# First expert pair's rows placed by one-hot matmuls from x on chip, and last pair's rows placed and all rows summed in PSUM, in a one-core hybrid encoder layer

## Chip, cores and metric

The kernel runs on one core of a Trainium2 chip. The metric is the device time of one execution in microseconds (us). Everything is float32. The kernel is written engine by engine with semaphores, so each engine executes its own list in the order in which the code is written: PE (matmul), DVE (vector), ACT (scalar), POOL (GpSimd) and SP, whose queue issues most of the transfers.

## The reference, cut to what matters

512 prompt tokens and 64 sample tokens of width 1024 (576 rows, five tiles: four of 128 rows and one of 64) pass one encoder layer. The change touches its last part, the mixture of experts, and the final norm:

```python
# router: top-1 of 4 groups, then top-2 of the 8 experts of that group
g_idx = jnp.argmax(glog, axis=-1)
top_v, top_i = lax.top_k(elog_g, 2)
gate = jax.nn.softmax(top_v, axis=-1) * g_w[:, None]
e_idx = g_idx[:, None] * 8 + top_i
# per expert, on the rows that chose it (h = rms_norm(x)); 32 experts, FF = 512
y = (silu(h @ w_gate[e]) * (h @ w_up[e])) @ w_down[e]
x = x + sum_over_the_2_experts(gate * y)
y_out = rms_norm(x, final_norm_g)
```

## The kernel before, in words

Attention, the HGRN2 recurrence, memory attention and the router take the first 640 us of the span. Then come 16 "pairs" (PAIRS). A pair is two experts, each with room for 64 rows (CAP), so its operand is one 128-row tile: columns 0 to 63 are the rows of one expert and 64 to 127 those of the other. Rows past 64 of an expert go into "over" passes after pair 8. Experts 0 to 3 are always pairs 0 and 1, so these two can start before the order of the rest is known.

**Weights.** Each pair needs six parts of 2 MB (two gate, two up, two down), 16 x 6 in all, streamed by SP through ten slots (PART, `load_part`). Part q goes into the slot of part q-10, so it waits until PE has read that one (`freed`): up parts of pair i free the slots for the gate parts of pair i+2, down parts of pair i those for its up parts, gate parts of pair i+1 those for its down parts. Pair 1's down parts are an exception: they go in halves, the first when PE has read half of pair 0's gate parts (`g_half`), the second after `g_full` (L1098 to L1104). Pair 15's parts go in quarters (`load_quarters`).

**Rows.** As the last projection gives x tile by tile (`proj_N(16, ...)`), ACT stores it to DRAM (`store_x`), PE turns it for the router (`turn_x`, `router`), and DVE chooses the experts (`choose`). `ranks` counts on PE which place a row has in its expert. For the first two pairs, DVE makes one-hots of the places (`near_slots`, `near_values`) and PE multiplies them with the token numbers (`near_tokens`), which gives the list of rows. POOL gathers these rows of x from DRAM (L1233) into `xg`, PE turns them (`turn_rows`) and DVE copies them, times the norm's gain, into `xgT` (`copy_rows`). Lists for the other pairs come from a second chain: about 9 us of small DVE steps up to `order_ready` (L1961 to L1990), 8 us more up to the one-hots (L2001 to L2057), ten matmuls on PE (`all_lists`, L916), and `read_lists` (`table_ready`), after which POOL may gather pair 2's rows.

**A pair** on PE: gate and up (`from_rows`, 16 matmuls each), `turn_rows` of the next pair, `turn_h`, down (`by_both`). ACT takes exp of the gate, DVE makes the swish (`swish_rows`), copies the turned product, and adds the gated result to the rows (`drain_rows`); the rows a token has for its first expert carry x itself (`own_rows`). POOL scatters the 128 rows to DRAM (`expert_rows`, one half for each of a token's two experts) and gathers the rows of pair i+3. PE's down of pair i waits until DVE has drained pair i-1 (`y_cp`).

**The end.** After pair 15's scatter has landed, SP and ACT load both halves of `expert_rows` (ten transfers), DVE adds them (L2122), ACT squares and sums, POOL takes the inverse root, DVE scales (L2127), SP stores.

Of the kernel before, what the change touches and what calls it, by code (L numbers as in the profile page):

```python
# [14 lines left out]
F32 = mybir.dt.float32  # L15
I32 = mybir.dt.int32
# [31 lines left out]
NOROW = 4096  # L48
PAIRS = NE // 2
# [55 lines left out]
def encoder(nc, a, outs):  # L105
# [4 lines left out]
    with ExitStack() as ctx:  # L110
# [6 lines left out]
        banks = [ctx.enter_context(nc.psum_tensor(f"bank{i}", [P, 512], F32)) for i in range(6)]  # L117
# [73 lines left out]
        x_sb = area(XZ, NT, 1024)  # L191
        hmT = area(Z2, KC, TOK)
# [16 lines left out]
        xgT = area(44032, KC, P)  # L209
        eG = area(OZ, 512)  # L210
        hET = area(OZ + 512, 4, P)
        hE = area(OZ + 1024, 512)
        hE_rows = hE.rearrange("p (d k) -> p k d", k=4)
        gS2 = area(OZ + 1536, 512)
        yS = [area(OZ + 2048 + 1024 * i, 1024) for i in range(2)]
        xo = area(OZ + 4096, 1024)
        xo_rows = xo.rearrange("p (d k) -> p k d", k=KC)

        yg = [[area(1024 * (2 * t + k), 1024) for k in range(2)] for t in range(NT)]
# [59 lines left out]
        r_g1 = early(NT)  # L279
        r_sum = early(NT)  # L280
# [3 lines left out]
        r_t = early(NT, NE)  # L284
        r_sel = early(NT, NE)
        before = early(NT + 1, NE)
        place = early(NT, NE)
# [6 lines left out]
        rank4 = early(NT, 4)  # L294
        own4 = early(NT, 4)
        valid4 = early(2, NT, 4)
        pair4 = early(2, NT, 2)
        list4 = early(2, NT, 2, 2)
# [3 lines left out]
        kept = scratch(OZ + 2048, OZ + 5376)  # L302
        oh = kept(2, NT, NE)
        hot_s = kept(2, NT, P)
        order_cmp = area(OZ + 2048 + 2 * NT * NE, NE, NE)
        cmp_e = area(OZ + 2048 + 2 * NT * NE, OVER, NE)
        squares4 = area(OZ + 2048 + 2 * NT * (NE + P), 1024)
        hot_p = kept(2, NT, NB // 2)
        lists = kept(2, NT, 4, NB // 2)
        lo_f = kept(2, NT)  # L310
        hi_f = kept(2, NT)
        eo = kept(OVER)
        cmp_p = kept(OVER)
        npf = kept(1)
# [3 lines left out]
        r_x4 = kept(NT, 4)  # L318
# [15 lines left out]
        half4 = fixed(4)  # L334
# [4 lines left out]
        ocol = fixed(4)  # L339

# [49 lines left out]
        near_hot, near_full, near_ready, near_std = (sem(f"near_{n}") for n in ("one_hots", "lists_full", "rows_ready", "std_ready"))  # L390
        hot_ready, lists_full, table_ready, order_ready = (sem(f"list_{n}") for n in ("one_hots", "full", "table_ready", "order_ready"))
# [13 lines left out]
        over_done = sem("over_passes_done")  # L405
        gf_ld = sem("final_gain_loaded")
        yg_ld = [sem(f"y_rows_loaded{t}") for t in range(NT)]
        fsum, fssq, frstd, fin_ready = (sem(f"final_{n}") for n in ("sum", "ssq", "rstd", "ready"))
        fin_st = sem("final_stored")

        A = PsumRing(banks[0:3], a_full, a_free)
# [49 lines left out]
        def _(pe):  # L461
# [345 lines left out]
            def near_tokens(a, b):  # L807

                for k in range(2):
                    for t in range(a, b):  # L810
                        rows = TILES[t][1]
                        ins = mm(near_list, hot_s[0:rows, k, t, :], list4[0:rows, k, t].rearrange("p v i -> p (v i)"), start=k == 0 and t == 0,
                                 stop=k == 1 and t == SAMPLE, skip_group_check=True)
                return ins
# [24 lines left out]
            router(3, HIGH)  # L839
            turn_x(4, 1)  # L840
            router(4, HIGH)
            pe.wait_ge(near_hot, 1)
            near_list = A.open(pe)[:, 0:4]
            mark["near"] = A.filled % 3
            near_tokens(0, 2)
            pe.wait_ge(sel_ready, 2)
            ranks(2, NT)
            pe.wait_ge(near_hot, 2)
            near_tokens(2, NT).then_inc(near_full, 1)

            pe.wait_ge(v_free, V.filled)
            pe.wait_ge(a_free, A.filled)
# [22 lines left out]
            def from_rows(S, n, bank, w, signal, half_read=None):  # L875

                for k in range(KC):
                    if k % 4 == 0:
                        pe.wait_ge(S.xT_cp, 2 * n + k // 4 + 1)
                    for j in range(2):  # L880
                        own = slice(CAP * j, CAP * (j + 1))
                        ins = mm(bank[own, :], xgT[:, k, own], w[j][:, k, :], start=k == 0, stop=k == KC - 1)  # L882
# [41 lines left out]
            for i in range(PAIRS):  # L924
# [20 lines left out]
                if i == 0:  # L945
                    all_lists()
# [1210 lines left out]
```

## Time and profile before

| | |
|---|---|
| Time, median of 3 | 1164.77 us (1164.1 to 1165.12) |
| The profiled execution | 1165.38 us, its span 1163.6 us |
| PE, PEld, DVE, ACT, POOL busy | 89%, 46%, 39%, 16%, 10% of the span |
| Read from HBM | 273.34 MB, of which 96 expert parts of 2048 KB and six more for the over pass |
| The chain that ended last | PE 69%, DMA 18%, DVE 6%, SP's queue 4% |

The span can be read in three stages: up to about 650 us PE is nearly always busy and the transfers mostly idle; from about 662 us to 1120 us the 16 DMA engines are full; the last 30 us follow the last weights. In a table of `--windows` kind the columns are the stretch, its length, then the busy time of PE, PEld, DVE, ACT and POOL with the count of instructions, the granted TensorE clock (1.00 is 2.4 GHz, 0.50 is 1.2 GHz), the busy share of the DMA engines and GB/s. In a timeline they are start, duration, engine, line, operation, out<-in with shapes, count, and in brackets the idle time before and who ended it. A float32 matmul counts as two PE instructions in the trace and as one in the listings of order.

### The profile page before, as it was taken

To read this page: it belongs to the slowest core of one execution; us is meant where nothing else is said; L and a number is where in the kernel's file an instruction comes from. 1 tells how busy PE (TensorE), PEld (TensorE's weight loads), DVE (VectorE), ACT (ScalarE), POOL (GpSimd) and SP (SyncE) were. 2 spreads that over 40 slices of the span, in tenths; PEclk is the share of its full clock that TensorE was granted. 3 is DMA by queue.
4 is the path that set the end of the run, shared out by engine and by line. 5 is a ranking of instruction groups with operands and counts; after the bars stand their busy time and mean duration, and the time that the engine had idled before them with its cause. 6 is when DMAs were issued, how large, how long until landed. Compare 5 with 4: busy or idle time off the path is not lost.

```text
span 1163.6 us, 11497 instructions
## 1 busy us (share of the span) xinstructions
PE 1032.4 (89%) x4528; PEld 540.7 (46%) x4528; DVE 458.5 (39%) x770; ACT 186.1 (16%) x486; POOL 113.1 (10%) x167
## 2 busy tenths in 40 slices
PE   6999999999999999999998699987876889887880
PEld 3577744555445446777656343333332233333320
DVE  4169645563664024013227743322222233322224
ACT  0156233433113101012101000000000000000001
POOL 1200001132016000000000010010000000100002
PEclk9999999999999999999998699999989899989995
DMA  8221130312233433212085599999999999999977
GB/s 254 73 73 54 45 123 1 134 52 82 74 108 103 177 145 145 73 57 89 1 355 200 220 397 427 427 427 426 428 427 426 422 427 427 426 427 427 413 297 251
DMA packets 56548, 277.50 MB, mean 238 GB/s; under 512 B 13360, under 2 KB 15280, under 8 KB 44336
## 3 DMA queue, kind: packets, MB, share of 16 engines
q1 hardware_dynamic: 43648, 256.01, 54.7%
q10 hardware_dynamic: 7808, 11.32, 2.7%
q0 software_dynamic: 5040, 9.45, 2.2%
q8 instruction: 36, 0.59, 0.2%
q14 instruction: 16, 0.13, 0.0%
HBM read 273.34 MB, written 18.61 MB: 251 GB/s over the span
## 4 chain that ended last, share of the span: by engine, by line
PE 69%; DMA 18%; DVE 6%; SPq 4%; issue 2%; ACT 0%; POOL 0%; ACTq 0%; DVEq 0%; POOLq 0%
PE bank L497 23%; DMA arena<-in_exp_w_down_dram 15%; PE bank L485 13%; PE bank L882 12%; PE bank L872 6%; SPq L1089 4%; PE bank L501 2%; PE bank L747 2%; PE score_pair L721 2%; PE bank L635 1%; DVE arena L1675 1%; DMA arena<-expert_rows 1%; PE score_pair L551 1%; PE bank L585 1%; DMA arena<-in_w_in_dram 1%
## 5 line engine op out<-in xcount | busy, mean ns | idle before, releaser
L497 PE MATMUL bank<-arena 128*128 128x512 f32 x640 | 285.0, 599 | 2.6 <-DMA arena<-in_w_in_dram 1.9
L882 PE MATMUL bank<-arena 128*64 128x512 f32 x1024 | 238.3, 622 | 38.5 <-issue 35.2
L497 PEld LDWEIGHTS bank<-arena 128*128 128x128 f32 x640 | 119.7, 191 | 147.0 <-issue 145.5
L882 PEld LDWEIGHTS bank<-arena 128*64 128x64 f32 x1024 | 83.4, 143 | 190.6 <-issue 189.4
L485 PE MATMUL bank<-arena 128*128 128x288 f32 x640 | 156.1, 406 | 0.0
L872 PE MATMUL bank<-arena 128*64 128x512 f32 x512 | 119.5, 621 | 26.6 <-DMA arena<-in_exp_w_down_dram 19.5
L485 PEld LDWEIGHTS bank<-arena 128*128 128x128 f32 x640 | 121.4, 190 | 33.8 <-issue 0.4
L1298 ACT ACTIVATE arena<-bank 128x512 f32<-128x512 f32 (+6 forms) x135 | 61.7, 493 | 378.3 <-PE bank L497 112.5
L872 PEld LDWEIGHTS bank<-arena 128*64 128x64 f32 x512 | 39.9, 142 | 95.1 <-issue 83.5
L1521 ACT ACTIVATE arena<-bank,arena 128x512 f32<-128x512 f32 x17 | 11.7, 687 | 428.3 <-PE bank L882 404.4
L2045 DVE SCALAR_TENSOR_TENSOR arena<-bank,arena 128x512 f32<-128x512 f32 x34 | 25.5, 751 | 109.8 <-PE bank L872 102.8
L2028 DVE TENSOR_SCALAR arena<-arena 128x512 f32<-128x512 f32 x17 | 7.3, 427 | 131.9 <-ACT arena L1521 131.9
L2030 DVE RECIPROCAL arena<-arena 128x512 f32<-128x512 f32 x17 | 57.0, 3353 | 0.6
L1237 POOL DMA_INDIRECT expert_rows<-arena,ints x17 | 17.2, 1010 | 384.3 <-DVE arena L2045 383.7
L1795 DVE TENSOR_TENSOR arena<-arena,bank 128x512 f32<-128x512 f32 x16 | 11.0, 688 | 87.0 <-PE bank L497 68.1
L1142 POOL TENSOR_SCALAR arena<-arena 128x1 f32<-128x1 f32 (+4 forms) x31 | 8.9, 288 | 373.4 <-ACT arena L1403 225.1
L1712 DVE SCALAR_TENSOR_TENSOR arena<-arena,score_pair 128x256 f32<-128x256 f32 (+4 forms) x20 | 15.3, 764 | 64.7 <-PE score_pair L551 49.3
L2035 DVE SCALAR_TENSOR_TENSOR arena<-bank,arena 128x512 f32<-128x512 f32 x17 | 12.8, 751 | 59.4 <-PE bank L882 55.6
L1775 DVE SCALAR_TENSOR_TENSOR arena<-arena,bank 128x128 f32<-128x128 f32 x68 | 23.7, 348 | 29.5 <-PE bank L635 26.5
L1825 DVE TENSOR_REDUCE arena<-score_pair 128x4 f32<-128x1024 f32 (+1 forms) x5 | 6.1, 1225 | 69.1 <-PE score_pair L721 69.1
L501 PE MATMUL bank<-arena 128*64 128x256 f32 x256 | 29.5, 382 | 0.5 <-DVE arena L1837 0.5
L1413 ACT ACTIVATE arena<-arena 128x128 f32<-128x128 f32 (+4 forms) x40 | 21.3, 534 | 35.5 <-DVE arena L1716 35.5
(295 smaller groups left out, 928.1 us busy)
## 6 DMA issues: line engine op xcount, KB each, us to landing
arena<-in_exp_w_gate_dram SPq DMA_DIRECT2D x30, 2048.0 KB, 33.0
arena<-in_exp_w_up_dram SPq DMA_DIRECT2D x30, 2048.0 KB, 37.7
arena<-in_exp_w_down_dram SPq DMA_DIRECT2D x28, 2048.0 KB, 34.7
arena<-in_w_in_dram SPq DMA_DIRECT2D x7, 2048.0 KB, 8.5
out_dram<-arena SPq DMA_DIRECT2D x4, 1024.0 KB, 10.5
arena<-in_w_mem_k_dram SPq DMA_DIRECT2D x2, 2048.0 KB, 10.3
arena<-in_w_mem_v_dram SPq DMA_DIRECT2D x2, 2048.0 KB, 8.6
arena<-in_w_out_dram SPq DMA_DIRECT2D x2, 2048.0 KB, 12.7
```

The lines of the kernel that those rows point to most:

```text
L485: ins = mm(b[:, 0:HALF], w[:, k, c * P:(c + 1) * P], src[:, k, t0:t0 + HALF], start=k == 0, stop=k == KC - 1)
L497: ins = mm(b[:, :], x, w[:, k, :], start=k == 0, stop=k == KC - 1)
L501: ins = mm(b[rows * half:rows * (half + 1), 0:256], x, w[:, k, 256 * half:256 * (half + 1)], start=k == 0, stop=k == KC - 1)
L721: ins = mm(o, qmT[:, 2 * h + c, t0:t0 + rows], keys[:, 2 * h + c, :], start=c == 0, stop=c == 1)
L747: ins = mm(b[:, c * P:c * P + rows], vals[:, m, j * P:(j + 1) * P], pT[:, 2 * (j // 2) + m, 0:rows], start=m == 0, stop=m == 1)
L872: ins = mm(bank[own, :], x[:, k, own], w[j][:, k, cols], start=k == 0, stop=k == nk - 1)
L882: ins = mm(bank[own, :], xgT[:, k, own], w[j][:, k, :], start=k == 0, stop=k == KC - 1)
L1089: sp.dma_start(pass_weights(i)[2 * which + j][:, ks, :], weights_of(which, e[j])[:, ks, :]).then_inc(late_ld[which][k], 16)
L1298: A.done(f(dst, get(b), ACT.Copy))
L1775: ins = stt(out=dst, in0=state(g), scalar=EB[:, h, g:g + 1], in1=inc, op0=ALU.mult, op1=ALU.add)
L2030: v.reciprocal(eG, eG).then_inc(S.chain, 1)
L2045: stt(out=y[:, cols], in0=banks[3 + half][:, :], scalar=gates, in1=own[:, cols], op0=ALU.mult, op1=ALU.add).then_inc(S.y_cp, 1)
```

## The change

It has two parts, and the moves that make room for them.

**First pair.** `ranks` now puts -1024 (PICKED) on the diagonal of its triangle, so that the rank of a chosen row is marked by itself, and DVE makes the one-hots of a tile in one comparison (`near_rows`; three calls for tiles 0-1, 2, 3-4 in place of `near_slots` and `near_values` for tiles 0-1 and 2-4). PE multiplies x, still in SBUF and read in columns, by the one-hot: `place_x(t, ks)` adds tile t's part of the first pair's operand, already turned, into two banks; eight matmuls of 128 columns for each of five tiles. Neither the gather, nor `turn_rows` of pair 0, nor the DVE order chain stands ahead of pair 0 any more. The gather of pair 0 is still issued, for `own_rows`. DVE now goes on with `order_ready`'s chain, then `swish_rows` of pair 0, `copy_rows` of pair 1, the second chain, `all_lists`, `read_lists`, `passes_needed`, and only then `drain_rows` of pair 0. PE runs `all_lists` in pair 1 (after its up matmuls, ahead of `turn_rows` of pair 2) instead of in pair 0. `copy_rows` of pair 0 waits for all stores of x, and SP's part (1, 3) for PE's reading of x tile 0.

**Last pair.** The 1152 rows of `expert_rows` are zeroed in DRAM early (four transfers of SP, from a zeroed stretch of SBUF, when `pool_c` is 2, ahead of `load_unit(2)`). Pair 15 is not scattered. Its 128 rows stay in SBUF; DVE makes a one-hot of their tokens (`hot_last`), and PE adds, in PSUM and for each of the five token tiles, the one-hot product (`place_last`) and the two loaded halves multiplied by the identity (`add_loaded`): two plus four matmuls of 512 columns a tile, 30 in all. The loads now wait for pair 14's scatter only, and all ten are issued by SP. ACT and DVE read the sums from PSUM.

PE around pair 0 before (L804 ranks, L778 turn_x, L792 router, L812 near_tokens, L857 turn_rows, L882 gate and up, L916 all_lists, L864 turn_h, L872 down):

```order
L792 MATMUL score_pair<-arena 128x36 x4
L778 MATMUL bank<-arena 128x64 x4
L792 MATMUL score_pair<-arena 64x36 x4
L812 MATMUL bank<-arena 128x4 x4
L803 MATMUL bank<-arena 128x128
L804 MATMUL bank<-arena 128x96
L812 MATMUL bank<-arena 128x4 x6
L857 MATMUL score_pair<-arena 128x128 x8
L882 MATMUL bank<-arena 64x512 x32
L857 MATMUL score_pair<-arena 128x128 x8
L916 MATMUL bank<-arena 128x100 x10
L864 MATMUL bank<-arena 128x128 x4
```

The same place now (L829 place_x, L821 near_tokens, L912 gate and up):

```order
L829 MATMUL banks<-arena 128x128 x4
L787 MATMUL banks<-arena 128x64 x4
L829 MATMUL banks<-arena 128x128 x4
L801 MATMUL score_pair<-arena 64x36 x4
L829 MATMUL banks<-arena 128x128 x16
L821 MATMUL score_pair<-arena 128x2 x6
L812 MATMUL banks<-arena 128x96
L813 MATMUL banks<-arena 128x64
L829 MATMUL banks<-arena 128x128 x16
L821 MATMUL score_pair<-arena 128x2 x4
L912 MATMUL banks<-arena 64x512 x32
```

The turning of gathered rows ahead of the first gate and up is gone, and 40 matmuls of 128 columns have come in.

PE in pair 1 now, from its gate and up to pair 2's (L887 turn_rows of pair 2, L946 all_lists, L894 turn_h, L902 down):

```order
L912 MATMUL banks<-arena 64x512 x32
L946 MATMUL banks<-arena 128x100 x10
L887 MATMUL score_pair<-arena 128x128 x8
L894 MATMUL banks<-arena 128x128 x4
L902 MATMUL banks<-arena 64x512 x16
```

Between the lists and down stands the turning of pair 2's rows, which are gathered by these lists.

DVE from the end of the order chain to the drain of pair 0, now, with the steps inside each chain left out (L2068 to L2077 swish_rows, L2020 copy_rows, L2116 the last one-hots, L2130 to L2138 read_lists, L2154 the end of passes_needed, L2111 drain_rows):

```order
L2063 CAST ints<-arena 128x32
L2068 TENSOR_SCALAR arena<-arena 128x512
L2077 COPY arena<-banks 128x512
L2020 TENSOR_TENSOR arena<-score_pair,arena 128x512 x2
L2116 TENSOR_TENSOR arena<-arena 128x640
L2130 TENSOR_SCALAR ints<-banks 128x25
L2138 TENSOR_SCALAR arena<-banks 128x25
L2154 CAST ints<-arena 128x1
L2111 SCALAR_TENSOR_TENSOR arena<-banks,arena 128x512 x2
L2068 TENSOR_SCALAR arena<-arena 128x512
```

Before, the second chain stood ahead of pair 0's swish; the swish of pair 1 (the last row) now stands behind the lists' reading and pair 0's drain.

PE after the last down now (L936 down by quarters, L1016 place_last, L1025 add_loaded; before, its list ends with down):

```order
L936 MATMUL banks<-arena 64x512 x16
L1016 MATMUL banks<-arena 128x512
L1016 MATMUL score_pair<-arena 128x512
L1016 MATMUL banks<-arena 128x512 x4
L1025 MATMUL banks<-arena 128x512 x4
L1025 MATMUL score_pair<-arena 128x512 x4
L1025 MATMUL banks<-arena 128x512 x8
L1016 MATMUL banks<-arena 64x512 x2
L1025 MATMUL banks<-arena 64x512 x4
```

The 30 matmuls follow down, those of the loaded rows behind the placed ones of the first four tiles.

The diff, cut to its core:

```diff
+            def place_x(t, ks):
+                rows = TILES[t][1]
+                for k in ks:
+                    ins = mm(first_rows[k // 4][:, (k % 4) * P:(k % 4 + 1) * P], x_cols[t][0:rows, k, :], near_hots[0:rows, t, 0, :],
+                             start=t == 0 and k % 4 == 0, stop=t == SAMPLE, skip_group_check=True)
+                return ins
             router(3, HIGH)
+            pe.wait_ge(sel_ready, 2)
+            ranks(2, 3)
+            pe.wait_ge(a_free, A.filled)
+            pe.wait_ge(near_hot, 1)
+            place_x(0, LOW)
             turn_x(4, 1)
+            place_x(0, HIGH).then_inc(x0_read, 1)
             router(4, HIGH)
+            place_x(1, range(KC))
+            pe.wait_ge(near_hot, 2)
+            place_x(2, range(KC))
+            near_tokens(0, 3)
+            pe.wait_ge(sel_ready, 3)
+            ranks(3, NT)
+            pe.wait_ge(near_hot, 3)
+            for ks in (LOW, HIGH):
+                place_x(3, ks)
+                place_x(4, ks).then_inc(SP_.tx_full, 1)
+            pe.wait_ge(near_hot, 4)
+            near_tokens(3, NT).then_inc(near_full, 1)
...
-            pe.wait_ge(xg_ld[0], 16)
-            turn_rows(SP_, xg_rows[0])
...
+                if i == 0:
+                    pe.wait_ge(near_std, 1)
+                if i == 1:
+                    all_lists()
                 if i + 1 < PAIRS and i != OVER_AFTER:
                     pe.wait_ge(xg_ld[(i + 1) % 3], 16 * ((i + 1) // 3 + 1))
                     turn_rows(SP_, xg_rows[(i + 1) % 3])
-                if i == 0:
-                    all_lists()
...
+            for half in range(2):
+                pe.wait_ge(SP_.y_cp, 2 * PAIRS - 1 + half)
+                for t in range(2):
+                    place_last(t, half)
+            for t in range(2, SAMPLE):
+                for half in range(2):
+                    place_last(t, half)
+            for t in range(SAMPLE):
+                add_loaded(t)
+            pe.wait_ge(fin_ready, 1)
+            for half in range(2):
+                place_last(SAMPLE, half)
+            add_loaded(SAMPLE)
...
+            sp.wait_ge(pool_c, 2)
+            y_flat = y_dram.rearrange("(p r) n -> p (r n)", p=P)
+            for c in range(4):
+                sp.dma_start(y_flat[:, 2304 * c:2304 * (c + 1)], area(OZ, 2304)).then_inc(y_zero, 16)
...
-            sp.wait_ge(y_st[1], 16 * (PAIRS // 2))
+            sp.wait_ge(y_st[1], 16 * (PAIRS // 2 - 1))
...
+            swish_rows(SP_, 0, 0, near[:, 1, 0:1])
+            copy_rows(SP_, 1, turned)
...
             all_lists()
+            read_lists()
+            passes_needed()
+            n.settle()
             for i in range(PAIRS):
-                swish_rows(SP_, i, 0, near[:, 1, 0:1] if i == 0 else table[:, 1, i:i + 1])
+                if i > 0:
+                    swish_rows(SP_, i, 0, table[:, 1, i:i + 1])
+                    if i + 1 < PAIRS and i != OVER_AFTER:
+                        copy_rows(SP_, i + 1, turned)
```

## Rows read from the trace of the kernel before

**Rows 1.** Table of stretches: busy times, granted clock, DMA share, GB/s.

```profile
646.50:661.72 15.22, 8.55 (x26) 3.83 (x28) 13.95 (x48) 0.07 (x1) 2.31 (x2) 0.52 0.24 75
684.38:707.66 23.28, 22.50 (x110) 8.33 (x108) 8.67 (x9) 1.72 (x2) 2.41 (x3) 1.00 0.99 404
752.00:1120.00 368.00, 304.08 (x1360) 118.02 (x1356) 109.47 (x112) 22.41 (x26) 25.41 (x30) 0.94 1.01 424
```

**Rows 2.** Timeline, 630 to 662 us: the router's end and pair 0's start.

```profile
630.04 1.08 PE L792 MATMUL score_pair<-arena 128*128 128x36 f32 x8
633.74 0.16 DVE L1892 TENSOR_REDUCE arena<-arena 128x2 f32<-128x8 f32 x1
...
638.47 0.42 DVE L1906 TENSOR_TENSOR arena<-arena 128x32 f32<-128x32 f32 x2
642.48 2.99 PE L812 MATMUL bank<-arena 128*128 128x4 f32 x12 [2.36 <-DVE arena L1932]
651.25 1.97 PE L857 MATMUL score_pair<-arena 128*128 128x128 f32 x8 [5.78 <-DMA arena<-x_rows,ints]
654.22 0.18 DVE L1990 CAST ints<-arena 128x32 int32<-128x32 f32 x1
655.14 16.84 PE L882 MATMUL bank<-arena 128*64 128x512 f32 x64 [1.92 <-DVE arena L1997]
661.72 4.24 SPq L1104 DMA_DIRECT2D arena<-in_exp_w_down_dram  x4
```

**Rows 3.** The chain that ended last, merged: start, length, what.

```profile
538.53 3.57 PE bank L747 x32
595.05 6.87 PE bank L497 x16
684.34 13.73 PE bank L882 x64
773.19 8.78 PE bank L872 x32
```

**Rows 4.** Timeline, 672 to 693 us: pair 0's lists, table, gather.

```profile
672.91 2.88 PE L916 MATMUL bank<-arena 128*128 128x100 f32 x20
677.25 7.09 PE L872 MATMUL bank<-arena 128*64 128x512 f32 x32 [0.78 <-DVE arena L2037]
677.90 0.18 DVE L2071 TENSOR_SCALAR arena<-bank 128x25 f32<-128x25 f32 x1
678.85 0.99 POOL L1233 DMA_INDIRECT arena<-x_rows,ints x1 [29.55 <-DVE arena L2071]
681.81 0.15 DVE L2087 CAST ints<-arena 128x1 int32<-128x1 f32 x1
684.38 0.82 SPq L1047 DMA_DIRECT2D arena<-in_exp_w_up_dram  x2
692.44 3.35 DVE L2030 RECIPROCAL arena<-arena 128x512 f32<-128x512 f32 x1
```

**Rows 5.** DMA issues, us to landing: at 679 us, 684 us, all 18.

```profile
arena<-x_rows,ints POOLq DMA_INDIRECT x1, 7.3
arena<-x_rows,ints POOLq DMA_INDIRECT x1, 10.1
arena<-x_rows,ints POOLq DMA_INDIRECT x18, 15.3
```

**Rows 6.** The chain that ended last, from 1133 us.

```profile
1133.06 0.75 DVE arena L2045
1139.44 13.20 DMA arena<-expert_rows
1156.25 1.06 ACT arena L1554
```

**Rows 7.** Timeline, POOL near 36 us.

```profile
35.66 0.54 POOL L1167 MEMSET arena<- 128x20 f32 x1
```

**Rows 8.** Table of stretches, 36 to 48 us.

```profile
36.00:48.00 12.00, 12.00 (x57) 5.92 (x57) 3.23 (x17) 1.50 (x4) 0.20 (x1) 1.00 0.01 1
```

More of the change, by code:

```diff
@@ L48 @@
 NOROW = 4096
+PICKED = 1024.0
 PAIRS = NE // 2
@@ L191, in encoder @@
         x_sb = area(XZ, NT, 1024)
+        x_cols = [x_sb[:, t, :].rearrange("p (d k) -> p k d", k=KC) for t in range(NT)]
         hmT = area(Z2, KC, TOK)
@@ L405, in encoder @@
         over_done = sem("over_passes_done")
+        y_zero, count_ready, hot_last_ready = sem("y_rows_zeroed"), sem("token_count_ready"), sem("last_one_hot_ready")
+        f_full = sem("tokens_summed")
         gf_ld = sem("final_gain_loaded")
         yg_ld = [sem(f"y_rows_loaded{t}") for t in range(NT)]
-        fsum, fssq, frstd, fin_ready = (sem(f"final_{n}") for n in ("sum", "ssq", "rstd", "ready"))
+        fssq, frstd, fin_ready = (sem(f"final_{n}") for n in ("ssq", "rstd", "ready"))
         fin_st = sem("final_stored")
+        summed = [bank_pairs[0], pair, bank_pairs[1], bank_pairs[2], bank_pairs[0]]
         A = PsumRing(banks[0:3], a_full, a_free)
@@ L807, in near_tokens @@
             def near_tokens(a, b):
[L809 to L813, printed above, removed]
+                for t in range(a, b):
+                    rows = TILES[t][1]
+                    for i in range(2):
+                        ins = mm(near_list[:, 2 * i:2 * i + 2], near_hots[0:rows, t, i, :], near_vals[0:rows, t, :], start=t == 0 and i == 0,
+                                 stop=t == SAMPLE, skip_group_check=True)
+                return ins
+            def place_x(t, ks):
+                rows = TILES[t][1]
+                for k in ks:
+                    ins = mm(first_rows[k // 4][:, (k % 4) * P:(k % 4 + 1) * P], x_cols[t][0:rows, k, :], near_hots[0:rows, t, 0, :],
+                             start=t == 0 and k % 4 == 0, stop=t == SAMPLE, skip_group_check=True)
                 return ins
@@ L980, in _, with place_last, add_loaded @@
                     turn_rows(SP_, xg_rows[(i + 1) % 3])
+            pe.wait_ge(hot_last_ready, 1)
+            def place_last(t, half):
+                t0, rows = TILES[t]
+                mm(summed[t][0:rows, half, :], hot_last[:, t0:t0 + rows], yS[(PAIRS - 1) % 2][:, 512 * half:512 * (half + 1)],
+                   start=True, stop=False, skip_group_check=True)
+            def add_loaded(t):
+                rows = TILES[t][1]
+                pe.wait_ge(yg_ld[t], 32)
+                for half in range(2):
+                    for k in range(2):
+                        ins = mm(summed[t][0:rows, half, :], ident[0:rows, 0:rows], yg[t][k][0:rows, 512 * half:512 * (half + 1)],
+                                 start=False, stop=k == 1, skip_group_check=True)
+                ins.then_inc(f_full, 1)
+            for half in range(2):
[8 more added lines that the diff above has]
+            pe.wait_ge(fin_ready, 1)
+            for half in range(2):
+                place_last(SAMPLE, half)
+            add_loaded(SAMPLE)
         @block.sync
@@ L1547, in _ @@
                     over_loop(act, over_pair)
-            act.wait_ge(y_st[0], 16 * (PAIRS // 2))
-            act.wait_ge(y_st[1], 16 * (PAIRS // 2))
-            for t, (t0, rows) in enumerate(TILES):
-                act.dma_start(yg[t][1][0:rows, :], y_dram[TOK + t0:TOK + t0 + rows, :]).then_inc(yg_ld[t], 16)
             for t, (_, rows) in enumerate(TILES):
-                act.wait_ge(fsum, t + 1)
-                f(yg[t][1][0:rows, :], yg[t][0][0:rows, :], ACT.Square, accum_out=ssq[0:rows, 17 + t:18 + t]).then_inc(fssq, 1)
+                act.wait_ge(f_full, t + 1)
+                f(yg[t][1][0:rows, :].rearrange("p (h n) -> p h n", h=2), summed[t][0:rows, :, :], ACT.Square,
+                  accum_out=ssq[0:rows, 17 + t:18 + t]).then_inc(fssq, 1)
         @block.vector
```

206 lines of the change are left out of this document (100 added, 106 removed).

## Prediction

> **What bounds the kernel now.** I read the page's busy slices first, then stretches, the chain that ended last, and the timeline at the two places of the change. From 752 to 1120 us the DMA engines have a busy share of 1.01 and move 424 GB/s, while PE is idle for 64 of 368 us: the weights' transfer sets the time there [rows 1]. From 684.38 us, while PE is still ahead of its weights, the share is 0.99 already. But from 646.5 to 661.72 us, it is 0.24: all slots are full and SP waits for the first half of pair 0's gate to be read. So what counts at the start is when that happens (661.72 us, the issue of L1104 [rows 2]), and whether the engines run dry later. At the end it is what lies behind the last weights: drain at 1133.06 us, scatter, load for 13.20 us, sums, norm, store [rows 6]. The profiled execution took 1165.38 us with a span of 1163.6, and is 0.6 us above the median; I sum on it and take 0.6 off.
>
> **Zeroed rows.** SP issues them when POOL's constants are ready, after 35.66 + 0.54 = 36.2 us [rows 7]. From 36 to 48 us the DMA share is 0.01 [rows 8]. 4.7 MB at 424 GB/s are 11.1 us, done by 47.5 us. The weights behind them in SP's queue wait for PE to have read its first unit, which by the idle engines isn't before 48 us, and PE then has the second unit to work on. Cost 0; if the writes took double, still 0.
>
> **Pair 0's start.** A 128-column matmul costs 3.57 us / 16 = 0.223 us at the full clock (32 instructions are 16 matmuls) [rows 3]. PE is through the last projection at 630.1 us. Router 1.1 us (its row: 1.08), ranks of tile 2 0.65, four placings 0.9, turning 0.5, four placings 0.9, router 0.7: the fifth tile's logits are full at 634.8 us, some 2 us later than before. DVE takes them and chooses for tiles 3 and 4, 5.15 us from 633.74 to 638.89 before [rows 2], now 635.1 to 640.3. Placing tiles 1 and 2 (16 x 0.223 = 3.6 us) and six near_tokens lie on PE beside that. Then ranks 0.7, the comparison 0.5, placing tiles 3 and 4 16 x 0.223 = 3.6, four near_tokens. Those cost 2.99 / 6 = 0.5 us each in the row at 642.48 us, where the clock was 0.5 [rows 2]; at the full clock I take 0.3. Sum 646.3, with semaphores 647 us, against 655.14. Half of the gate's matmuls are a quarter of the 13.73 us of a pair's 64 instructions at the full clock [rows 3], 3.4 us; before, the clock was 0.52 on average over this stretch [rows 1], and it took 6.6. SP issues at 650.7 us instead of 661.72: **-11.0 us** at the start of the full stream. The bounds: -12 if no hop costs anything; -2.5 with PE at 1.2 GHz in the last placings (rival C).
>
> Parts (1,2) and (1,3) change places and wait for the logits and for tile 0's placing, both by 635 us, when part (1,0), issued at 630.2, still fills the engines: 0.
>
> **Pair 0 and what it pushes back.** The shift is handed on to the end only if the engines never run dry. From 647: gate and up to 660.8. DVE's order chain runs from 646.5 for the 8.7 us that it took before (to 654.22 plus 0.18 [rows 2]), so the swish starts at 655.4, waits a little for up, and down 0 runs from 663.7 to 670.8 (7.09 us [rows 4]). Each issue up to there follows the one before closely enough: 0.
>
> The second list chain used to be hidden beside pair 0's gate and up. Its lists are now summed on PE in pair 1. Pair 1's gate and up take 13.8 us, to 684.6; the ten list matmuls 2.9 (20 instructions [rows 4]), to 687.5; the table is ready 1.0 later and POOL's gather starts 0.8 after that (677.90 + 0.18 to 678.85 [rows 4]): 689.3 us. Only when it has landed can PE turn pair 2's rows, and turn_h and down of pair 1 stand behind that in PE's list. Before, this gather was issued in pair 0 and PE never waited for it. Now nothing hides it. Its landing is the price that the trace doesn't fix: alone it took 7.3 us at 679 and 10.1 at 684 us, and the median of all 18, most of them behind a scatter, is 15.3 [rows 5]. The new one stands alone, but with about 15 us of weights queued ahead, as at no place of before. I take 10.1: 699.4 us. PE has then been idle for 12 us, so its clock will be at 1.2 GHz: turning 1.97 us (the row at 651.25 [rows 2]), turn_h 1.3, DVE's copy 0.7, down 8.78 as after another long wait (773.19 [rows 3]): it ends at 712.3 us. Parts (3,2) and (3,3) wait for it.
>
> How long can the engines go on? At 670.8 us six parts' worth is still to come before those two: 12.58 MB at 424 GB/s are 29.7 us; with three gathers and a scatter of 0.52 MB each 5.0 more: dry at 705.5 us. From 684.38 to 707.66 us the rate was 404 [rows 1], which makes it 707. Idle **+7.0 us**, of which the bounds are +4 (landing at 696.6, then the swish of pair 1 is what is late) and +12 (15.3).
>
> The Trainium skill ("DMA: Bandwidth & Descriptors", Queues, rings and completion order) says that each engine takes turns between its queues packet by packet; a lone gather would then land in some 4.5 us by its fixed 2 us and its rate, an estimate of mine from that page's figures. The landings in rows 5 speak against it, and by the rule the sum would be that of rival A.
>
> After that DMA catches up and DVE and POOL have no late work: nothing in pairs 2 to 14 changes.
>
> **The end.** The last quarter of down and the two drains stay as they are. Placing may start when the first drain is done (1133.06 + 0.75, so 1133.9 us). Thirty matmuls of 512 columns at 6.87 / 8 = 0.859 us [rows 3] are 25.8 us; the sample tile's, with 64 output rows, have as many columns and cost the same. PE has been busy before, so I take the full clock. Loads: SP issues them when pair 14's scatter has landed, behind the last quarters in the same queue, and these have landed before 1133 us. 4.7 MB are 11.1 us, so the first tile lands by 1135.3 and the last by 1144. PE wants the first at 1133.9 + 8 x 0.859 = 1140.8 and one more each 3.4 us: hidden. All sums are in PSUM at 1159.7 us. Before, the last sum was ready at 1156.25 us, when ACT squared it [rows 6]. Square, inverse root, scaling and store follow as before, 7.4 us; a read of 1024 columns from PSUM I price at up to 0.2 us more in all. **+3.5 us**, bounds +2.8 and +4.5. Scatter, DVE's adds and the load go, but what takes their place is longer: PE must do six passes over every row behind the drain, four of which (the loaded rows) didn't need it.
>
> Sum: -11.0 + 7.0 + 3.5 = -0.5 us. 1165.38 - 0.5 - 0.6 gives **1164.3 us**: no change that can be told (about 0.2%, 2.3 us, is what a measurement of this kernel tells from none).
>
> **Rivals.**
> A, faster: the gather lands in 7.3 us or less. Then pair 1's swish is late: table 688.5, passes_needed 2.6 (681.96 less 678.08, less 1.3 for the copy that stood between [rows 4]), pair 0's drain 1.6 (two of 0.75 [rows 6]), swish 5.3 around the 3.35 us reciprocal [rows 4]: 698.1, down ends at 709.4, idle 4.0. With the start 0.5 us better the sum is -11.5 + 4.0 + 3.5 = -4.0: 1160.8. For it: the 7.3 us; against it: that one had a short queue ahead. 34%.
> B, slower: the gather lands like the others, 15.3 us: down ends at 717.5, idle 12, sum +4.5: 1169.3. For it: the queue is as deep as in the steady pairs; against: no scatter ahead. 16%.
> C, slower: PE is at 1.2 GHz when tiles 3 and 4 are placed. Before, it was there from 634 us on, after small router matmuls and waits. Then ranks, 16 placings, four near_tokens cost 0.7 + 3.6 + 0.8 more and the first half gate 3.4: the start gives only -2.5, and the sum is +8.0: 1172.8. It decides from the point where PE idles before sel_ready 3. Against: the placings of tiles 1 and 2 keep it at work until 640 us. 10%.
> D: the end at 1.2 GHz, 25.8 us more, and 1190. PE has no long pause before it. 2%.
> That the change doesn't do what it says: the listings show the gather gone from pair 0's way. 2%, with the times of before.
>
> **How the numbers follow.** Forecast 36%. The case without effect is within 0.2% too, but the forecast's upper edge passes it, so same stays at 36%. Faster: A, 34%. Slower: B, C, D and that edge, 30%. The range goes from A's better half to between B and C: 1159.3 to 1171. The forecast's own, with an idle time of 5 to 9 us: 1162.3 to 1166.3.
>
> **What the profile would show.** Pair 0's gate starting near 647 us at a clock near 1, and no turning before it; a wait of about 10 us of PE for x_rows in pair 1, the clock at 0.5 after it, and a dip in DMA share near 706 to 712 us; 30 matmuls in the last 30 us and ACT's last square 3 to 4 us later behind the last drain than before (23.2 us). If the last quarter of down lands 4 us earlier, both start terms hold. Wrong it would be if the dip isn't there (faster), or if pair 0 starts after 650 us (slower).

## The result and the profile after

The changed kernel takes **1178.3 us** (median of 4 runs, 1175.55 to 1180.25), the kernel before 1164.64 beside it: a ratio of 1.0118, 95% interval 1.0101 to 1.0134. The forecast, 1164.3 with a range to 1171, was wrong, its range too. The profiled execution took 1176.76 us with a span of 1175.0, against 1163.6 before: 11.4 us to find. (The medians are 13.7 us apart: the profiled execution of before is 0.7 us above its median, that of the changed kernel 1.5 us below. No profile shows the other 2.3 us.)

First pair 0's start, the timeline of the changed kernel (start, length, engine, line, what; [idle before it and who ended that]):

```profile
630.89 2.14 PE L829 MATMUL banks<-arena 128*128 128x128 f32 x8
635.56 1.07 PE L801 MATMUL score_pair<-arena 128*64 128x36 f32 x8
636.55 7.90 PE L829 MATMUL banks<-arena 128*128 128x128 f32 x32
644.29 1.40 PE L821 MATMUL score_pair<-arena 128*128 128x2 f32 x12
646.71 8.88 PE L829 MATMUL banks<-arena 128*128 128x128 f32 x32 [0.52 <-DVE arena L1990]
657.40 15.80 PE L912 MATMUL banks<-arena 128*64 128x512 f32 x64
662.95 4.25 SPq L1170 DMA_DIRECT2D arena<-in_exp_w_down_dram  x4
```

L829 places rows of x. Eight instructions took 2.14 us while the clock was still up, 0.27 us each, where the forecast had 0.11 (0.223 a matmul, which is two instructions). The gate (L912) starts at 657.4 instead of 647, and 2.3 us later than before [rows 2]. SP issues at 662.95, 1.2 us later than before, not 11.0 earlier.

The clock over this stretch (us, PE busy, granted clock, DMA share, GB/s):

```profile
632.00:634.00 2.00, 2.00 (x12) 0.97 0.97 410
634.00:636.00 2.00, 2.00 (x11) 0.50 0.98 410
638.00:640.00 2.00, 2.00 (x10) 0.50 0.73 266
642.00:644.00 2.00, 2.00 (x10) 1.00 1.08 455
646.00:648.00 2.00, 1.48 (x7) 0.88 0.96 410
648.00:650.00 2.00, 2.00 (x9) 0.50 0.08 33
```

The clock falls to 1.2 GHz twice: at 634 us, when PE has been busy without a gap, and at 647 us, after a wait of 0.52 us. At 642 to 644 us, with the clock at 2.4 GHz, it does 10 instructions in 2 us, as many as at 638 to 640 with 1.2: something other than the clock holds a placing back.

Then pair 1, where the changed kernel sums the lists (L946), gathers pair 2's rows (L1303) and turns them (L887):

```profile
696.43 2.98 PE L946 MATMUL banks<-arena 128*128 128x100 f32 x20
701.26 0.99 POOL L1303 DMA_INDIRECT arena<-x_rows,ints x1 [39.96 <-DVE arena L2138]
712.45 1.97 PE L887 MATMUL score_pair<-arena 128*128 128x128 f32 x8 [13.04 <-DMA arena<-x_rows,ints]
716.06 7.09 PE L902 MATMUL banks<-arena 128*64 128x512 f32 x32 [0.79 <-DVE arena L2077]
723.18 0.81 SPq L1112 DMA_DIRECT2D arena<-in_exp_w_up_dram x2
```

PE waits 13 us for a gather that lands 11.2 us after POOL's issue. Down 1 ends at 723.1, where the forecast had 712.3: 10.4 of these 10.8 us are the late gate. The rest is small because misses cancel: the gather's issue is 1.6 us later behind the gate than forecast and its landing takes 1.1 us more, but the turning and down 1 take 2.2 us less, as down 1 runs at the full clock (7.09 us) where the forecast had 8.78. The transfers pay for it. Of before, then of the changed kernel (us, granted clock, DMA share, GB/s):

```profile
640.00:730.00 90.00, 0.88 0.86 351
700.00:730.00 30.00, 1.00 1.01 430
```

```profile
640.00:730.00 90.00, 0.84 0.78 316
700.00:730.00 30.00, 0.77 0.80 326
```

Against the 1.01 of full transfer, 90 x (0.86 - 0.78) = 7.2 us of transfer time are lost, 6.3 of them after 700 us. From 730 us both run at 1.01, and the last quarter of down comes 8.0 us later (1139.81 against 1131.84). The end:

```profile
1139.81 1.94 PE L936 MATMUL banks<-arena 128*64 128x512 f32 x8 [0.39 <-DMA arena<-in_exp_w_down_dram]
1141.01 1.54 DVE L2111 SCALAR_TENSOR_TENSOR arena<-banks,arena 128x512 f32<-128x512 f32 x2 [6.09 <-PE banks L936]
1141.90 1.10 PE L1016 MATMUL banks<-arena 128*128 128x512 f32 x2 [0.16 <-DVE arena L2111]
1164.53 3.64 PE L1025 MATMUL banks<-arena 64*64 64x512 f32 x8
```

ACT's last square starts at 1168.21, 27.2 us behind the drain (the row of L2111); before, it was 23.2 (1133.06 to 1156.25, [rows 6]). So 4.0 us; with the 8.0 it makes 12.0, of which 0.6 come back behind the square (6.8 us to the end, 7.4 before): 11.4.

The zeroed rows show as four writes, with a DMA share of 0.58 from 30 to 60 us where it was 0.20, and nothing behind them comes later.

### The profile page after: what moved, and what is told of

It reads as the page before. It is cut to its first block, busy times and chain, and to the rows that moved or that the text cites. A ratio compares the mean times of both kernels' runs of the same rounds, so it can differ in the third digit from the quotient of the medians.

```text
span 1175.0 us, 11766 instructions
## 1 busy us (share of the span) xinstructions
PE 1076.0 (92%) x4664; PEld 565.7 (48%) x4664; DVE 452.4 (39%) x758; ACT 185.6 (16%) x486; POOL 109.1 (9%) x168
## 4 chain that ended last, share of the span: by engine, by line
PE 76%; DMA 13%; SPq 4%; DVE 4%; issue 2%; another core or an unknown queue 1%; ACT 0%; DVEq 0%; POOL 0%; ACTq 0%; POOLq 0%
PE banks L506 23%; PE banks L494 13%; PE banks L912 13%; DMA arena<-in_exp_w_down_dram 11%; PE banks L902 7%; SPq L1155 4%; PE banks L510 2%; PE banks L829 2%; PE banks L756 2%; PE score_pair L730 2%; PE banks L644 1%; PE banks L1025 1%; DVE arena L1745 1%; PE score_pair L560 1%; DMA arena<-x_rows,ints 1%
## 5 line engine op out<-in xcount | busy, mean ns | idle before, releaser
L506 PE MATMUL banks<-arena 128*128 128x512 f32 x640 | 285.2, 599 | 2.5 <-DMA arena<-in_w_in_dram 1.8
L912 PE MATMUL banks<-arena 128*64 128x512 f32 x1024 | 237.1, 620 | 35.8 <-issue 34.3
L506 PEld LDWEIGHTS banks<-arena 128*128 128x128 f32 x640 | 119.8, 191 | 146.9 <-issue 145.4
L912 PEld LDWEIGHTS banks<-arena 128*64 128x64 f32 x1024 | 81.1, 143 | 188.3 <-issue 187.1
L494 PE MATMUL banks<-arena 128*128 128x288 f32 x640 | 156.1, 406 | 0.0
L902 PE MATMUL banks<-arena 128*64 128x512 f32 x512 | 119.2, 620 | 21.2 <-DMA arena<-in_exp_w_down_dram 11.8
L494 PEld LDWEIGHTS banks<-arena 128*128 128x128 f32 x640 | 121.4, 190 | 33.8 <-issue 0.4
L1371 ACT ACTIVATE arena<-banks 128x512 f32<-128x512 f32 (+6 forms) x135 | 61.6, 492 | 378.7 <-PE banks L506 110.5
L902 PEld LDWEIGHTS banks<-arena 128*64 128x64 f32 x512 | 38.4, 142 | 91.1 <-issue 77.7
L2111 DVE SCALAR_TENSOR_TENSOR arena<-banks,arena 128x512 f32<-128x512 f32 x34 | 25.4, 750 | 101.6 <-PE banks L902 95.5
L2068 DVE TENSOR_SCALAR arena<-arena 128x512 f32<-128x512 f32 x17 | 7.2, 426 | 119.0 <-ACT arena L1594 119.0
L2075 DVE SCALAR_TENSOR_TENSOR arena<-banks,arena 128x512 f32<-128x512 f32 x17 | 12.8, 751 | 60.4 <-PE banks L912 57.4
L1845 DVE SCALAR_TENSOR_TENSOR arena<-arena,banks 128x128 f32<-128x128 f32 x68 | 23.6, 348 | 29.5 <-PE banks L644 26.5
L887 PE MATMUL score_pair<-arena 128*128 128x128 f32 x128 | 19.3, 296 | 14.1 <-DMA arena<-x_rows,ints 13.0
L510 PE MATMUL banks<-arena 128*64 128x256 f32 x256 | 29.5, 382 | 0.5 <-DVE arena L1907 0.5
## 6 DMA issues: line engine op xcount, KB each, us to landing
out_dram<-arena SPq DMA_DIRECT2D x4, 1024.0 KB, 10.4
```

The lines of the kernel that those rows point to most:

```text
L494: ins = mm(b[:, 0:HALF], w[:, k, c * P:(c + 1) * P], src[:, k, t0:t0 + HALF], start=k == 0, stop=k == KC - 1)
L506: ins = mm(b[:, :], x, w[:, k, :], start=k == 0, stop=k == KC - 1)
L510: ins = mm(b[rows * half:rows * (half + 1), 0:256], x, w[:, k, 256 * half:256 * (half + 1)], start=k == 0, stop=k == KC - 1)
L902: ins = mm(bank[own, :], x[:, k, own], w[j][:, k, cols], start=k == 0, stop=k == nk - 1)
L912: ins = mm(bank[own, :], xgT[k // 4][:, k % 4, own], w[j][:, k, :], start=k == 0, stop=k == KC - 1)
L1371: A.done(f(dst, get(b), ACT.Copy))
```

## Experiments

The kernel before was timed beside each group of runs: medians 1164.1 to 1164.7. Theory from the first: the placings are slow by themselves and at a low clock (8 us), and the end costs 4.

**only_start** and **only_end** halve the change: the first is the changed kernel with the old end, the second the old kernel with the new end.

> The changed kernel with the end of the kernel before (pair 15 scattered, both halves loaded and added by DVE, no rows zeroed). Theory (the two parts' costs add: the start costs 8 us, by a late pair 0 and a dry stretch of the DMA engines in pair 1; the end 4 us): 1164.6 + 8 = 1172 to 1175 us, pair 1's down ending near 723 us. Rival (the zeroed rows or something between the parts does it, the start alone is harmless): 1164 to 1167 us.

> The kernel before with the end of the changed one alone. Theory: 30 matmuls of 0.86 us behind the first drain, 1164.6 + 4 = 1168.6 us, with a spread as small as before's, since the start is untouched. Rival (the end is harmless, all is lost at the start): 1164 to 1165.5 us.

Only the start: 1173.81 us, ratio 1.0079 (1.0062 to 1.0097); only the end: 1168.01, 1.0029 (1.0016 to 1.0041). The halves add up, 9.7 and 3.9 of 13.7 us. The placings read as in the changed kernel, and ACT's last square of only_end comes 27.2 us behind its drain at 1133.48.

**rows_in_chunks.** A placing's stationary operand took every eighth column of x, a step of 32 bytes. Here it takes 128 neighbouring ones, and pair 0's gate and up weights, and its gain, are read in the matching order.

```diff
-        x_cols = [x_sb[:, t, :].rearrange("p (d k) -> p k d", k=KC) for t in range(NT)]
+        x_cols = [x_sb[:, t, :].rearrange("p (k d) -> p k d", k=KC) for t in range(NT)]
...
+                if i == 0 and m < 4:
+                    src = a[which_name[m // 2]][0, e].rearrange("(k p) n -> p k n", p=P)
```

> The changed kernel with x read by place_x as eight stretches of 128 neighbouring columns instead of every eighth column; pair 0's gate and up parts are loaded, and its gain is taken, in the same order of rows. Theory (the weight loads with a step of 32 bytes take 0.335 us instead of 0.19, they hold the placings at 0.25 us an instruction, and this thin load lets the clock fall): placings of tiles 3 and 4 in 3.6 to 4.5 us instead of 8.9, pair 0's gate at 648 to 651 us, SP's next issue at 652 to 655 instead of 663, time 1167 to 1170 us, runs closer together. Rival (the clock falls for another reason, the step costs nothing): placings as before, 1175 to 1180 us.

1169.69 us (9 runs, 1165.25 to 1172.68), 1.0045 (1.0033 to 1.0058). The time is the expected one; the last placings (3.6 to 4.5 us expected) and a narrower spread didn't come. The placings with x in chunks:

```profile
634.88 3.84 PE L829 MATMUL banks<-arena 128*128 128x128 f32 x32
640.53 0.46 PE L812 MATMUL banks<-arena 128*128 128x96 f32 x2 [0.58 <-DVE arena L1979]
641.71 8.09 PE L829 MATMUL banks<-arena 128*128 128x128 f32 x32 [0.52 <-DVE arena L1993]
651.61 15.70 PE L912 MATMUL banks<-arena 128*64 128x512 f32 x64
```

The weight loads (PEld) of the first eight instructions, in the changed kernel and with x in chunks, both at the full clock:

```profile
630.86 1.98 PEld L829 LDWEIGHTS banks<-arena 128*128 128x128 f32 x8
631.72 0.97 PEld L829 LDWEIGHTS banks<-arena 128*128 128x128 f32 x8
```

Same tile, same count: the step doubles the load, by 0.13 us an instruction. It also goes with the first fall of the clock. From 634 to 640 us both kernels run placings of the same shape with PE busy; the changed kernel, then rows_in_chunks (columns as in [rows 1]):

```profile
634.00:640.00 6.00, 6.00 (x29) 5.71 (x29) 2.82 (x14) 0.00 (x0) 0.00 (x0) 0.50 0.90 322
634.00:640.00 6.00, 5.95 (x56) 5.70 (x54) 4.23 (x21) 0.00 (x0) 0.00 (x0) 1.00 1.01 400
```

The projection before ends up to 0.9 us apart from run to run, so count from the start of the router's last full tile (629.53, here 630.39): the gate starts 27.9 us behind it with the step and 21.2 in chunks, where the forecast had 16.9. So the step costs 6.7 us. The clock is the second fault: it still falls at 641.7 us, after 2-column products and waits of 0.58 and 0.52 us, and the last placing takes 8.09 us for the same 32 instructions.

**clock_kept** and **lists_moved.** The near lists go behind the placings (both); in their place come three products of 512 columns, meant for a free bank (clock_kept alone).

```diff
-near_tokens(0, 3)
+extra(2)        # each: mm(bank, ident, x_sb[:, 2, 0:512])
 pe.wait_ge(sel_ready, 3)
 ranks(3, NT)
+extra(1)
...
-near_tokens(3, NT).then_inc(near_full, 1)
+near_tokens(0, NT).then_inc(near_full, 1)
```

> The kernel with the rows of x read in chunks, and two more edits: the twelve products of the near lists (L821, 1.40 us before the last placings) go behind the placings, and in their place TensorE gets two extra products of 128x128 by 512 columns into a free bank ahead of the ranks and one behind them (0.86 us each at full clock; their result is not used). Theory (the second half of the lost start is the clock, which falls at 641.7 in the chunked kernel after a stretch of 2-column products and waits): the clock stays at 1.00 through the last placings, these take 3.8 to 4.2 us (32 instructions of 0.12) in place of 8.09, the near lists behind them 2.3 in place of 1.96, the first gate half 13.7 in place of 15.70; SP's issue after the gate comes 5 to 7 us before 657.05, and the time is 1163 to 1167 if the stall in pair 1 stays as long (the chunked kernel had 1169.7). Rival 1 (the low clock has nothing to do with what TensorE runs just before): the clock falls in the same place, the last placing takes 8 us, the near lists come behind it, the time is 1170.5 to 1172. Rival 2 (an earlier start is all eaten by the gather's landing): the clock stays up, SP's issue comes earlier, but the pair 1 stall grows by as much and the time stays at 1169 to 1170.

> The same as the kernel before it without the extra products: only the near lists are moved behind the placings. Theory (it is the columns TensorE streams that hold the clock): TensorE now waits from 638.5 to 640.5 for the ranks, the clock falls as in the chunked kernel (0.50 from about 641), the last placing takes 7.5 to 8.1 us, the lists behind it 3 to 4 us more, but a part of that lies beside VectorE's copies; 1169.5 to 1172. Rival (the order is what helped): the clock stays at 1.00 and the time is 1163 to 1167, as with the extra products.

clock_kept holds 2.4 GHz through the last placing:

```profile
636.98 1.88 PE L876 MATMUL banks<-arena 128*128 128x512 f32 x4
639.46 1.08 PE L876 MATMUL banks<-arena 128*128 128x512 f32 x2
640.37 4.31 PE L829 MATMUL banks<-arena 128*128 128x128 f32 x32
644.61 3.14 PE L821 MATMUL score_pair<-arena 128*128 128x2 f32 x20
647.68 16.57 PE L919 MATMUL banks<-arena 128*64 128x512 f32 x64
```

lists_moved, which has PE wait instead:

```profile
640.03 0.53 PE L812 MATMUL banks<-arena 128*128 128x96 f32 x2 [1.86 <-issue]
641.45 8.09 PE L829 MATMUL banks<-arena 128*128 128x128 f32 x32 [0.52 <-DVE arena L1992]
```

So the extra work ahead held the clock, not the order; it fills PE's wait as well, and no run tells the two apart. Behind the placings the clock falls all the same, during the 20 two-column products: 0.57 over 646 to 654 us. The gate takes 16.57 us, more than the 15.70 in chunks, and of the 3.8 us won in the last placing, 1.5 reach its issue, counted from the router. And clock_kept's time is 1170.61 us, 1.0049 (1.0032 to 1.0066), the same as with x in chunks. That is the time of rival 2, though PE's wait for the gather did not grow (12.85 us, 12.75 in chunks). The gate's issue comes 3.1 us earlier (653.99; 1.6 of them because the router was earlier), and so do the gather (692.30) and the turning; then down 1 takes 9.11 us at the low clock in place of 7.09, and the next issue stands at 716.06 against 716.99. Transfers of rows_in_chunks, then of clock_kept:

```profile
640.00:730.00 90.00, 0.85 0.85 344
700.00:730.00 30.00, 0.84 0.82 326
```

```profile
640.00:730.00 90.00, 0.87 0.85 342
700.00:730.00 30.00, 0.82 0.74 297
```

What is won early is lost after 700 us. (In clock_kept and all_mended the extra products fell into the bank of pair 0's first half and overwrite what is placed by then, so these two give wrong rows for pair 0; the instructions are the same, and mended_between below puts them right.) lists_moved took 1175.89 (1172.87 to 1176.02), 4 us above what was expected; its profiled run is the quickest of the four. There the 20 two-column products behind the placings take 4.51 us at the low clock, the gate starts 2.9 us later behind the router than in chunks, and the share over 640 to 730 is 0.82, worth 2.7 us; the rest of the 6 us over rows_in_chunks is open.

**lists_between.** The changed kernel with pair 1's lists between its gate and up, so that the gather lands beside up.

> The changed kernel with PE's list matmuls of pair 1 between its gate and up instead of behind up. Theory (the gather of pair 2's rows stands bare behind the lists and makes the DMA engines run dry): the gather is issued 7 us earlier, pair 1's down ends at 716 instead of 723, the dry stretch shrinks from 6 to 0 us, time 5 to 7 us below the changed kernel, 1170 to 1174 us. Rival (the engines don't miss what they lose there, since the stream is bound later): 1176 to 1180 us.

1172.31 us, 1.0068 (1.0051 to 1.0085): 6.0 us under the changed kernel.

```profile
690.08 2.98 PE L946 MATMUL banks<-arena 128*128 128x100 f32 x20
694.91 0.99 POOL L1303 DMA_INDIRECT arena<-x_rows,ints x1 [32.91 <-DVE arena L2138]
705.80 1.97 PE L887 MATMUL score_pair<-arena 128*128 128x128 f32 x8 [5.72 <-DMA arena<-x_rows,ints]
716.54 0.81 SPq L1112 DMA_DIRECT2D arena<-in_exp_w_up_dram x2
```

The landing is as long, 10.9 us from the issue, but the next issue comes 6.6 us earlier and the share after 700 us is 1.01 again.

**sums_shared.** The old kernel with the new end, in which DVE adds the two loaded halves of each tile as they land, so that PE has 20 products and not 30.

```diff
+tt(yg[t][0], yg[t][0], yg[t][1], ALU.add).then_inc(fsum, 1)     # DVE; slices of rows left out here and below
-    for k in range(2):
-        mm(summed[t], ident, yg[t][k], stop=k == 1)
+    mm(summed[t], ident, yg[t][0], stop=True)
```

> The kernel before with the changed end, in which VectorE adds the two loaded tables of each tile as they land (1.2 us each, five), so that TensorE has 20 products (10 that place, 10 that add) and not 30. Theory (the end was late because it put 25.8 us of TensorE's products behind the last drain): 10 products of 0.86 us fewer, the last square comes 8.6 us earlier than in the changed end alone, the time is 1168.0 - 8.6 = 1159.4, ratio 0.996. Rival (the landing of the ten loads sets the end, 13 to 14 us after an issue at 1131 at the latest, with VectorE's sums behind it): the last sum ends at about 1147 and the products behind it, at most 3 us; that would allow still earlier, so a rival time is only reached if the loads land later than 1152: 1163 to 1166.

1161.21 us (11 runs), 0.9976 (0.9966 to 0.9985): 6.8 us better than the new end, 1.8 less than expected. The rows show most of it:

```profile
1147.18 1.22 DVE L2170 TENSOR_TENSOR arena<-arena 64x1024 f32<-64x1024 f32 x1 [1.04 <-DMA arena<-expert_rows]
1148.33 1.27 DVE L2173 SCALAR_TENSOR_TENSOR arena<-banks,arena 128x1024 f32<-128x1024 f32 x1
1149.65 1.93 PE L996 MATMUL banks<-arena 128*64 128x512 f32 x4 [1.47 <-DVE arena L2173]
```

The last tile reuses tile 0's banks, which DVE empties only after its five sums: PE waits 1.5 us for it.

**All mends together.** all_mended has chunks, extra products, lists between and shared sums; mended_between is the same with the extra products in a bank that is really free.

> The changed kernel with all four mends: rows of x in chunks, extra products that hold the clock, pair 1's lists between its gate and up products, and VectorE's sums at the end. Theory (the parts add): from 1178.3, -8.6 for the chunks, -3 to -6 for the clock, -6 for the lists, -8.6 for the end: 1149 to 1153. Rival (transfers bound the middle once the start is early, so that the clock's and the lists' gains overlap): 1155 to 1158. If even the chunks and the lists overlap, 1159 to 1161.

> The kernel with all four mends, with the extra products written into a PSUM bank that holds nothing any more (in clock_kept and all_mended they fell into the bank of pair 0's first half rows and overwrote what tiles 0 to 2 had placed there). Nothing else differs, so theory and rival expect the same instructions and the same time: 1154 to 1158 (all_mended 1155.86), 0.992 to 0.994 of the kernel before. If the bank mattered to the time (a shared write of one bank by placings and extra products), the last placings would take other than 4.3 us and the time would move by under 1 us.

1155.86 and **1156.04 us** (5 runs each), mended_between 0.9924 (0.9910 to 0.9938) of the kernel before: the change, mended, is 8.7 us faster than the kernel that it was meant to beat. The sum of the parts was expected at 1149 to 1153, with 3 to 6 us for the clock and 8.6 for the end. With what the parts measured (8.6 for the chunks, 6.0 for the lists, 6.8 for the end, -0.9 for the extra products) it is 1157.8, within the runs' spread of 1156.0: the parts add, and what is missing is the clock's share and a part of the end's. Three more runs take the start apart.

> As the kernel before it, but pair 1's lists stand ahead of its gate product and not between gate and up. VectorE has their input ready at 677.4, TensorE would be there at 668.2 and waits 9 us. Theory (what costs is that TensorE stands still with all slots of weights full while the gather lands; its 10.9 us after the lists must lie beside two products of 7 us): gather issue at about 682 in place of 687, landing 693, no wait at the turning (694.3), next issue of down weights some 4 us earlier, gate 1's and up 1's 12 and 5 us later; the transfers' idle time of about 1 us goes, 0 to 2 us faster, 1153 to 1156. Rival (the 9 us wait for VectorE drains the queue of weights, as the 12.8 us wait did in the kernel with the rows in chunks): 2 to 6 us slower, 1158 to 1162.

> The mended start (chunks, extra products, lists between) with the kernel before's own end. Theory (parts add): mended_between without its better end, which is worth 1164.2 - 1161.2 = 3.0 us, so 1158 to 1160, 0.995 of the kernel before: the start part of the change is worth 5 us once its two faults are gone. Rival (the gain of all_mended is mostly its end, since the gather eats the start): 1162 to 1164.

> mended_between without the three extra products and with the near lists in their old place, so that the last placings run at 1.2 GHz again (8.1 us in place of 4.3). Theory (an earlier start is worth its time only once pair 1's wait no longer drains the transfers, which it does not with the lists between gate and up): SP's issue after the gate comes 2.5 to 3 us later (at about 658), and the time is 2 to 3 us longer, 1158 to 1159.5. Rival (the clock's 3 us are lost further on here as well, as they were between rows_in_chunks, 1169.7, and clock_kept, 1170.6): no difference, 1155.5 to 1157.

mended_first: 1156.47, no difference from mended_between, and between what theory and rival expected; PE waited less than thought (1.4 us, not 9), since pair 0's down lies ahead of the lists:

```profile
676.37 3.90 PE L953 MATMUL banks<-arena 128*128 128x100 f32 x20 [1.36 <-DVE ints L2132]
```

start_mended: 1159.95, 0.9955 (0.9942 to 0.9969), so by the medians 4.8 us of the 8.7 are the start's and the end brings 3.9 (3.0 in sums_shared). But its five runs fall into two groups, 1156.65 and 1156.96, then 1159.95 to 1160.45, and the profiled one is the first. In it the clock stays at 2.4 GHz behind the placings too:

```profile
647.79 13.96 PE L919 MATMUL banks<-arena 128*64 128x512 f32 x64
651.49 4.35 SPq L1145 DMA_DIRECT2D arena<-in_exp_w_down_dram  x4
```

The issue is 0.8 us from the forecast's 650.7, and the share over 640 to 730 is 0.95 against 0.86 before, 8.1 us. mended_between has the same PE instructions up to here, a clock of 0.62 over 646 to 654 us and its issue at 655.54. So an early start can be worth its time; whether the slower group lost it in the gate is not shown, as only one execution has a profile.

mended_low_clock: 1156.77, 0.9936 (0.9922 to 0.9949), 0.7 above mended_between: the rival's time, so the extra products are worth nothing that these runs can tell. Its transfers have a share of 0.91 from 640 to 730 us, mended_between's 0.92. Down 1 of mended_low_clock, then of mended_between:

```profile
700.06 1.97 PE L887 MATMUL score_pair<-arena 128*128 128x128 f32 x8 [6.00 <-DMA arena<-x_rows,ints]
703.67 7.09 PE L902 MATMUL banks<-arena 128*64 128x512 f32 x32 [0.78 <-DVE arena L2079]
```

```profile
697.51 1.97 PE L894 MATMUL score_pair<-arena 128*128 128x128 f32 x8 [5.36 <-DMA arena<-x_rows,ints]
701.12 9.50 PE L909 MATMUL banks<-arena 128*64 128x512 f32 x32 [0.78 <-DVE arena L2086]
```

Here too the turning comes 2.5 us earlier and down 1 loses 2.4 at a lower clock. That this is where the gain goes is not shown: mended_first has neither the wait nor the low clock there, and the same time. Why the clock is low for the second alone, after a wait no longer than that of the first, no run here settles.

## Why the prediction was wrong, point by point

- **Pair 0's start failed**: "Placing tiles 1 and 2 (16 x 0.223 = 3.6 us)", and tiles 3 and 4 likewise, "-11.0 us". It measured +1.2. The 0.223 us came from L747 [rows 3], a product whose stationary operand lies in neighbouring columns; the new one's steps 32 bytes and takes 7.90 us for 16 matmuls, 0.49 each. rows_in_chunks shows the step as the cause: 3.84 us, and a gate 6.7 us earlier. Of the 12.2 us between 662.95 and the forecast's 650.7, 10.4 are the late gate and 1.8 its first half, 5.5 us from start to issue at the low clock where the forecast had 3.7. I took the duration from a row of the same shape and did not compare the layout of its operand.
- **The clock**, rival C at 10%, came true: 8.88 us for the last placing, a gate of 15.8 in place of 13.7. Its case against, "the placings of tiles 1 and 2 keep it at work until 640 us", fell: PE was busy until 646 us and was granted 1.2 GHz from 634. With the extra products the last placing takes 4.31 us, and the gate starts 18.9 us behind the router's last full tile, 2.4 less than in chunks and 2.0 more than forecast (18.2 to 18.8 in the four others that have them). In four of these five profiles the clock then fell near the gate's start.
- **Idle +7.0 us in pair 1 was right in kind, and its size with luck**: the transfers lost 6.3 after 700. The gather landed in 11.2 us, between the 10.1 taken and the upper bound, and down 1 gained that back by its full clock: the forecast took 1.2 GHz for it from the row at 773.19 "after another long wait", but the wait there was 2.36 us. In clock_kept, with the gate within 0.7 us of the forecast, down 1 is slow (9.11 us), and 8.1 us are lost after 700. lists_between shows the wait as the cause.
- The prediction's estimate of 4.5 us for a lone gather, from the Trainium skill ("DMA: Bandwidth & Descriptors", Queues, rings and completion order), is not what these traces show: this gather landed in 10.5 to 11.6 us in ten kernels and in 8.9 in mended_first. Which part of the estimate is off, the turns or the fixed time, no run separates.
- **The end +3.5 was right**: +4.0 in the trace, 3.9 in only_end. Zeroed rows 0: right, nothing behind them is later. After 730 us nothing changes: right.
- With the measured terms the prediction's own sum is +1.2 (the issue) + 6.3 (transfer lost after 700 us) + 4.0 = 11.5 us, against 11.4 in the profiled executions. C had -2.5 as its start: the column step on top of the low clock takes that to +1.2.

## What to carry to other kernels

When a new instruction is priced by a row of another, compare not only the shape but the step of each operand: here every eighth column doubled a weight load. Where transfers set the time, count the transfer time lost over the stretch (length times missing share) rather than how much earlier a stage starts: in clock_kept the share over 640 to 730 us stayed at 0.85, and so did the time. When a profiled execution is not the median one, look at the spread before a gain is called nothing. A sum moved to TensorE is only cheap if another engine does the part that needs no placing.

## What the runs showed of the hardware

- Eight loads of float32 weights of 128x128 took 1.98 us from columns 32 bytes apart and 0.97 from neighbouring ones, both at 2.4 GHz.
- PE, busy without a gap before and during it, was granted 1.2 GHz from 634 to 640 us with the placings that have the step, and 2.4 GHz with those that have not. PE's busy share in the profile didn't tell the two apart.
- At 1.2 GHz the step showed little: 32 placing instructions took 8.09 us in chunks and 8.88 with the step.
- The same PE instructions were granted a different clock in two kernels: over 646 to 654 us 1.00 in start_mended and 0.62 in mended_between.
- The first gather of a list behind SP's weights landed 10.5 to 11.6 us after its issue in ten kernels, wherever that stood (683 to 702 us). It was 8.9 us in mended_first at 682 us, and 7.3 at 679 and 10.1 at 684 us before [rows 5].
